# The 31-tap convolution of a recurrent block: all eight tiles on TensorE, in 32x32 diagonal blocks that GpSimd makes

## What is computed

```python
h = rms_norm(x, pre_mix_norm)
p_r, p_k, p_v, p_c, z_rwkv, z_conv = split(h @ w_in)          # w_in: 1024 x 7168
u, gate = split(p_c)
c = u * sigmoid(gate)                                         # 256 x 1024
c = conv(c, dw) + dw_b          # depthwise and causal: c[t, f] = sum_s dw[30 - s, f] * c[t - s, f], 31 taps
y_conv = silu(layer_norm(c)) @ w_conv_out
y_rwkv = recurrence(p_r, p_k, p_v, h)                         # a state of 64 x 64 per head, 16 heads
x = x + rms_norm((sigmoid(z_rwkv) * y_rwkv + sigmoid(z_conv) * y_conv) @ w_out)
```

## Time and profile before

| | us |
|---|---|
| device time, median of 3 runs | 1477.15 |
| lowest, highest | 1475.12, 1480.46 |
| span of the profiled execution | 1474.3 |
| TensorE busy in it | 1383.9 |
| VectorE, ScalarE, GpSimd busy | 1039.1, 760.6, 138.3 |
| mean granted TensorE clock | 0.964 of full |

### The profile page before, as it was taken

How to read it: one execution, slowest core, us unless ns; L and a number is a source line. 1 busy time by engine, 2 the same in 40 slices (tenths; PEclk the granted TensorE clock), 3 DMA queues, 4 the chain that set the end, 5 groups by cost and what they waited for, 6 DMA issues and landing times.

```text
span 1474.3 us, 30170 instructions
## 1 busy us (share of the span) xinstructions
PE 1383.9 (94%) x12477; PEld 1331.2 (90%) x12477; DVE 1039.1 (70%) x1684; ACT 760.6 (52%) x1256; POOL 138.3 (9%) x147
## 2 busy tenths in 40 slices
PE   6998999997798999998998899999999998899997
PEld 6997988896798999998997699999999888899997
DVE  5769899895686665547598967877455655678843
ACT  4584383335645544445467655444355455554432
POOL 2000000001101211001010002111010100221100
PEclk9999999798899999999999899999999999999999
DMA  7633510120163552853484254554656521555550
GB/s 251 188 101 128 173 57 2 61 87 30 66 201 105 186 185 91 264 192 120 139 249 132 79 172 144 180 191 150 209 163 195 173 86 58 169 174 171 185 187 30
DMA packets 204369, 211.06 MB, mean 143 GB/s; under 512 B 8594, under 2 KB 201898, under 8 KB 204090
## 3 DMA queue, kind: packets, MB, share of 16 engines
q1 hardware_dynamic: 202154, 200.87, 42.2%
q0 software_dynamic: 2000, 8.46, 1.9%
q10 hardware_dynamic: 96, 0.02, 0.0%
HBM read 207.70 MB, written 1.64 MB: 142 GB/s over the span
## 4 chain that ended last, share of the span: by engine, by line
PE 72%; DVE 18%; ACT 5%; issue 2%; DMA 1%; POOL 1%; SPq 0%; DVEq 0%; ACTq 0%; POOLq 0%
PE pb L413 19%; PE pb L415 19%; PE pb L414 19%; DVE w_lo L442 3%; DVE pj L1447 2%; PE pb L1942 1%; DVE sub L1375 1%; PE pb L399 1%; PE pb L2324 1%; ACT w_hi L436 1%; DVE x_lo L1223 1%; DMA raw<-in_ffn_w_down_dram 1%; PE pb L1984 1%; PE pb L2030 1%; PE pb L1931 1%
## 5 line engine op out<-in xcount | busy, mean ns | idle before, releaser
L442 DVE TENSOR_TENSOR w_lo<-raw,w_hi 128x1024 fp32r<-128x1024 f32 (+1 forms) x384 | 471.0, 1229 | 165.7 <-ACT w_hi L436 164.9
L413 PE MATMUL pb<-x_hi,w_hi 128*128 128x256 f32 x1968 | 564.2, 287 | 21.4 <-DVE w_lo L442 12.0
L436 ACT ACTIVATE w_hi<-raw 128x1024 fp32r<-128x1024 f32 (+1 forms) x384 | 394.7, 1040 | 345.3 <-PE pb L415 297.1
L414 PE MATMUL pb<-x_lo,w_hi 128*128 128x256 f32 x1968 | 560.1, 285 | 0.0
L415 PE MATMUL pb<-x_hi,w_lo 128*128 128x256 f32 x1968 | 559.8, 284 | 0.0
L413 PEld LDWEIGHTS pb<-x_hi,w_hi 128*128 128x128 f32 x1968 | 381.0, 194 | 26.5 <-DVE w_lo L442 17.8
L414 PEld LDWEIGHTS pb<-x_lo,w_hi 128*128 128x128 f32 x1968 | 381.1, 194 | 0.2
L415 PEld LDWEIGHTS pb<-x_hi,w_lo 128*128 128x128 f32 x1968 | 381.0, 194 | 0.0
L413 PE MATMUL pb<-act_hi,w_hi 128*128 128x256 f32 x528 | 149.6, 283 | 2.6 <-DVE w_lo L442 2.6
L415 PE MATMUL pb<-act_hi,w_lo 128*128 128x256 f32 x528 | 149.4, 283 | 0.0
L414 PE MATMUL pb<-act_lo,w_hi 128*128 128x256 f32 x528 | 149.4, 283 | 0.0
(11 more groups left out here) (312 smaller groups left out, 2109.2 us busy)
## 6 DMA issues: line engine op xcount, KB each, us to landing
raw<-in_ffn_w_up_dram SPq DMA_DIRECT2D x55, 1024.0 KB, 5.0
raw<-in_w_in_dram SPq DMA_DIRECT2D x28, 1024.0 KB, 5.1
raw<-in_ffn_w_down_dram SPq DMA_DIRECT2D x24, 896.0 KB, 4.8
raw<-in_ssd_w_in_dram SPq DMA_DIRECT2D x20, 1024.0 KB, 5.3
raw<-in_fox_w_in_dram SPq DMA_DIRECT2D x16, 1024.0 KB, 5.8
raw<-in_ffn_w_down_dram SPq DMA_DIRECT2D x12, 1024.0 KB, 5.5
raw<-in_ffn_w_gate_dram SPq DMA_DIRECT2D x11, 1024.0 KB, 5.1
raw<-in_ssd_w_out_dram SPq DMA_DIRECT2D x8, 1024.0 KB, 5.1
```

The source lines that it names most:

```text
L413: pe.matmul(o, w_hi[m][:, k, :], hi[:, k0 + k, :], start=first and k == 0, stop=False)
L414: pe.matmul(o, w_hi[m][:, k, :], lo[:, k0 + k, :], start=False, stop=False)
L436: act.activation(w_hi[m][:, 0:nk, :], raw[s][:, 0:nk, m * P:(m + 1) * P], ACT.Copy).then_inc(sem("w_hi_ready"), 1)
L442: dve.tensor_tensor(w_lo[m][:, 0:nk, :], raw[s][:, 0:nk, m * P:(m + 1) * P], w_hi[m][:, 0:nk, :].bitcast(F32), ALU.subtract).then_inc(sem( ...
```

## The change

The convolution no longer runs on VectorE at all, and no longer as 128x128 diagonals on TensorE.

- A 128x128 diagonal holds 128 useful numbers. It is replaced by blocks of 32x32, each a diagonal of 32 features, at row group a (of 4) and column group c (of 4) of the array. For that the features of u and gate are laid out otherwise: tile c of a unit of 512 features holds, on partitions 32a to 32a+31, the features 128a + 32c + i. So 16 blocks (a, c) take four tiles through one tap, and block (a, c) adds to bank 4 + a, partitions of column group c, where the features come out in their usual order. There are 31 taps x 16 blocks x 2 halves = 992 products.
- The blocks are made by GpSimd, 8 instructions (`tap_weights`), each of 8 (or 7) taps x 4 x 32 = 1024 (896) elements per partition: the product of a small identity and the taps' parameters, both read by broadcast. Two are made after `PAIRS_MADE`, ahead of GpSimd's two transfers, six after `GLU_MADE`; there are four buffers (in slots A and GATE), so from the fifth on each waits for the products of four groups before.
- TensorE runs all 992 products after `GLU_MADE` and ahead of the inverses, after a new wait for the first two `z` evacuations, which VectorE now does first. ScalarE only copies the eight sums (`conv_half`), to slot U.
- VectorE's `conv_taps` and ScalarE's diagonals (93 instructions) are gone. `scale_keys(1)` and the loop's other work stay.
- The layer `ug` reads its weight blocks with runs of 32 columns; the first block of a unit needs both halves of the load, and the buffer is freed as a whole after the fourth block, where each half was freed after its two.
- The rows of the convolution's parameters are loaded in the new order: 8 transfers with runs of 32 values instead of 2 with runs of 128. GpSimd makes the small identity at the start, 4 copies of 32x32.

```diff
         def raw_block(ly, s, nk, m):
+            if ly.name == "ug":
+                return raw[s][:, 0:nk, :].rearrange("p k (a c i) -> p k a c i", c=QUARTERS, i=CHUNK)[:, :, :, m, :]
+            return raw[s][:, 0:nk, m * P:(m + 1) * P]
@@ GpSimd
+            def tap_weights(i):
+                h, b = divmod(i, TAP_GROUPS)
+                t0, t1 = tap_range(b)
+                c0 = col["conv_dw"]
+                w = par[:, c0 + KC * t0:c0 + KC * t1].rearrange("p (t k) -> p t k", k=KC)[:, :, QUARTERS * h:QUARTERS * h + QUARTERS]
+                shape = [P, t1 - t0, QUARTERS, CHUNK]
+                if i >= 4:
+                    pool.wait_ge(sem("tap_summed"), i - 3)
+                pool.tensor_tensor(tap_blocks(i)[:, 0:t1 - t0], ident_q[:, :].unsqueeze(1).unsqueeze(1).broadcast_to(shape),
+                                   w.unsqueeze(3).broadcast_to(shape), ALU.mult).then_inc(sem("tap_ready"), 1)
+            pool.wait_ge(sem("dve_stages"), PAIRS_MADE)
+            for i in range(2):
+                tap_weights(i)
             pool.wait_ge(sem("lab_ready"), NCHUNK)
...
+            pool.wait_ge(sem("dve_stages"), GLU_MADE)
+            for i in range(2, 2 * TAP_GROUPS):
+                tap_weights(i)
             pool.wait_ge(sem("dve_stages"), INVERSES_MADE)
@@ ScalarE
+            def conv_half(h):
+                act.wait_ge(sem("tap_summed"), TAP_GROUPS * (h + 1))
+                for a in range(QUARTERS):
+                    k = QUARTERS * h + a
+                    act.activation(slot(CV)[:, k, :], pb[4 + a][:, 0:T], ACT.Identity, bias=par_col("conv_b", k)).then_inc(sem("conv_ready"), 1)
@@ VectorE
+            z_evac(0, Z_EARLY)
             substitute(done + 1, (done + SUB_TOTAL) // 2)
-            z_evac(0, Z_EARLY)
             z_rests(BANKS, BANKS + Z_EARLY)
             substitute((done + SUB_TOTAL) // 2, SUB_TOTAL)
...
-            conv_taps(0, DVE_EARLY - 3)
             scale_keys(1)
-            conv_taps(DVE_EARLY - 3, DVE_EARLY)
...
-                conv_taps(DVE_EARLY + sum(DVE_TAPS[:c]), DVE_EARLY + sum(DVE_TAPS[:c + 1]))
@@ TensorE
             pe.wait_ge(sem("dve_stages"), GLU_MADE)
-            for k in range(PE_TILES):
-                if k >= 2:
-                    pe.wait_ge(sem("conv_ready"), k - 1)
-                for s in range(CONV_TAPS):
-                    pe.wait_ge(sem("tap_ready"), CONV_TAPS * k + s + 1)
-                    mm(pb[4 + k % 2][:, s:T], diag[(CONV_TAPS * k + s) % NDIAG], slot(U)[:, k, 0:T - s],
-                       start=s == 0, stop=s == CONV_TAPS - 1, skip_group_check=True).then_inc(sem("tap_summed"), 1)
-            pe.wait_ge(sem("conv_ready"), PE_TILES)
+            z_out(Z_EARLY)
+            for i in range(2 * TAP_GROUPS):
+                h, b = divmod(i, TAP_GROUPS)
+                t0, t1 = tap_range(b)
+                pe.wait_ge(sem("tap_ready"), i + 1)
+                for tap in reversed(range(t0, t1)):
+                    shift = CONV_TAPS - 1 - tap
+                    for a in range(QUARTERS):
+                        if h and shift == 0:
+                            pe.wait_ge(sem("conv_ready"), a + 1)
+                        for c in range(QUARTERS):
+                            ins = mm(pb[4 + a][quarter[c], shift:T], tap_blocks(i)[quarter[a], tap - t0, c, :],
+                                     slot(U)[quarter[a], QUARTERS * h + c, 0:T - shift],
+                                     start=shift == 0, stop=tap == 0, skip_group_check=True)
+                ins.then_inc(sem("tap_summed"), 1)
+            pe.wait_ge(sem("conv_ready"), KC)
```

More of the change, by code:

```diff
@@ L72, in params_of @@
         n = flat.shape[0] // P
-        out.append((name, n, flat.rearrange("(n p) -> n p", p=P)))
+        rows = flat.rearrange("(n p) -> n p", p=P)
+        if name == "conv_dw":
+            rows = flat.rearrange("(n a c i) -> n c a i", a=QUARTERS, c=QUARTERS, i=CHUNK)
+        out.append((name, n, rows))
     return out
@@ L139, in build, with tap_range, tap_blocks @@
         y_lo = nc.alloc_sbuf_tensor_at("y_lo", [P, KC, T], F32R, offset=arena_base + 8 * (BK + 1) * T * 4)
-        PE_TILES, NDIAG, DIAG_LEAD = 3, 12, 8
-        diag = [slot(ZC)[:, i // 2, P * (i % 2):P * (i % 2) + P] for i in range(NDIAG)]
+        CV, LN_TMP = U, GATE
+        TAP_GROUPS = -(-CONV_TAPS // TAP_GROUP)
+        def tap_range(b):
+            return max(0, CONV_TAPS - TAP_GROUP * (b + 1)), CONV_TAPS - TAP_GROUP * b
+        def tap_blocks(i):
+            v = slot((A, GATE)[i % 4 // 2])[:, 4 * (i % 2):4 * (i % 2) + 4, :].rearrange("p a b -> p (a b)")
+            return v.rearrange("p (t c i) -> p t c i", c=QUARTERS, i=CHUNK)
         Z_EARLY, Z_CHUNK = 2, 2
-        DVE_TAPS = (4, 4, 3, 3, 3, 3)
-        DVE_EARLY = CONV_TAPS - sum(DVE_TAPS)
         LAB_BLOCK, SUB_BLOCK, SUB_STEPS = 5, 9, 2
@@ L320, in build @@
                     ly.free[half].append(occupant[s][half])
-                    occupant[s][half] = ("w_lo_ready", item + M_PER_UNIT // 2 * (half + 1))
+                    occupant[s][half] = ("w_lo_ready", item + (M_PER_UNIT if ly.name == "ug" else M_PER_UNIT // 2 * (half + 1)))
                 unit += 1
@@ L430, in act_head @@
                 act.wait_ge(sem(f"landed{s}{half}"), nth(ly, u, p, ly.landed[half]))
+                if ly.name == "ug" and half == 0:
+                    act.wait_ge(sem(f"landed{s}1"), ly.landed[1][u])
             if ly.name == "lora_in" and m == 2:
@@ L624, in _ @@
                 rows = slice(32 * b, 32 * b + 32)
+                link(pool.tensor_copy(ident_q[rows, :], ident[rows, rows]))
                 link(pool.tensor_copy(g_mask[rows, 0:CHUNK], tri[rows, rows]))
@@ L879, in _ @@
                 z_head(j)
[L880 to L885, removed]
+            for h in range(2):
+                conv_half(h)
             for i in range(CHUNK // INV_GROUP):
@@ L1436, in _ @@
             dve.nop().then_inc(sem("dve_stages"), 1)
-            def conv_taps(first, last):
-                for s in range(first, min(last, CONV_TAPS)):
-                    for k in range(PE_TILES, KC):
-                        w = par_col("conv_dw", KC * (CONV_TAPS - 1 - s) + k)
-                        o, c = slot(GATE)[:, k, :], slot(U)[:, k, :]
-                        if s == 0:
-                            go(ts(o, c, w, par_col("conv_b", k), ALU.mult, ALU.add))
-                        else:
-                            go(stt(o[:, s:T], c[:, 0:T - s], w, o[:, s:T], ALU.mult, ALU.add))
-                    sync()
             def mask_products(c):
```

56 lines of the change are left out of this document (25 added, 31 removed).

## The result

The change made the kernel slower: the median of four runs is 1503.28 us (1500.25 to 1507.48), against 1478.81 us (1475.12 to 1480.81) for the kernel before on the same chip. The ratio of the runs is 1.018, with a 95% interval of 1.015 to 1.021 (the two medians alone give 1.0165). The forecast was 1472.5 with a range of 1461 to 1489; the sign was wrong too. The profiled execution of the changed kernel has a span of 1498.5 us, 24.2 more than before.

The account below looks back on a forecast made before the run. VectorE bounds before the loop, TensorE's convolution up to the inverses, TensorE in the loop with waits and clock. Loop -7.9, inverses -1.2, first two blocks +4.0, parameters +0.5: -4.6 us, 1472.5; range 1461 to 1489.

Parts of the forecast that it names:

- TensorE's convolution: After `GLU_MADE`: 1984 records at 0.41 to 0.49 us a tap, 25 to 30 us, reaching the inverses at 219 to 224.
- Rival C: Tap products start only every 22 ns, as in L2094: 44 us, inverses at 237.7, sum +6.4 us, 1483.6; chance 0.13.
- Parameters: At the kernel's start: six more load issues on SyncE's queue delay TensorE's turns of the parameters by 0.5 us.
- The two early blocks: After `PAIRS_MADE`, at 127.2 us: two GpSimd blocks hold up VectorE's products, 4.0 us later; bounds 0 and 8.8.
- GpSimd's instruction: Each tap block of 1024 elements on GpSimd takes 2.3 us, at 2.1 ns an element; bounds 2.3 and 4.6.
- Rival B: GpSimd's blocks take 4.6 us each: sum +14.0 us, 1491.2; chance 0.14.
- Six late blocks: After `GLU_MADE`: six GpSimd blocks cost VectorE's slabs 8.2 us; `INVERSES_MADE` at 226.6, inverses start 1.2 us sooner.
- The loop: Chunk loop without VectorE's multiply-adds: TensorE's 2.8 us of waits and part of its time at 1.2 GHz vanish, gain 7.9 us.
- Edits at nothing: Parts counted as costing nothing, such as ScalarE's lost diagonals, later `ug` loads and 32-column runs in the splits.

Follow-up runs that it names:

- the bursts of 64 columns: The changed kernel with each tap product after the unshifted one over 64 columns instead of 226 to 255: taps 54 us against 55, span 1494.8 us.
- the first pair of profiles: The first profile each of the kernel before and the changed kernel: loop 114.8 and 107.8 us; in the second profiles 111.9 and 112.1 us.

## Why the prediction was wrong, step by step

- *TensorE's convolution* is the step that failed. It took the pace of 7.5 to 15 ns from bursts of 32 records and asked only whether the array could hold it for 1984. Nothing in the sum asked whether the instructions would come. They come at 14 ns each, 28 ns a record with its load, so 1984 records take 55.5 us, not 25 to 30. With that the path was wrong too: the forecast had the inverses wait for VectorE's substitution (226.6, measured 228.8), and they waited for the taps, until 253.9. The taps started 1.0 us after the GLU, where 0.8 was forecast.
- Of the forecast's 0.41 to 0.49 us a tap of four tiles, bursts at full width took 2.3 us for four taps, 0.57. That alone would have made 36 us: the array's pace was sized too short as well, beside the supply that was left out.
- *Rival C* had the direction, and its row, L2094 at 22 ns, was the nearest to the truth; it was given 0.13 because L2112 was faster. But a run of 32 says nothing of a run of 1984. With C's 9.8 us replaced by the measured 26.0 - 6.7 = 19.3, its sum is 0.5 + 4.0 + 19.3 - 7.9 = +15.9. The Trainium skill's floor of about 25 ns (TensorE: Matmul & The Clock Gate, Wait — 56ns, not 53.3ns?) is near the average of 28; as a floor it doesn't hold here, since records come 13 ns apart inside the bursts of 64 columns.
- *Parameters*: 0.5 forecast, bounds 0 and 2.3, measured 4.0. The step took the duration of an issue from transfers with whole rows, 0.39; with runs of 32 values it was 0.73 in the median, eight times, so SyncE's next parameter load was issued 5.5 us later (20.0 against 14.5), and TensorE waited 2.8 us for the last of them.
- *The two early blocks*: 4.0 forecast, 2.7 measured, mechanism right. VectorE's L463 took 2.99 us and its next large product (L1381) 3.67:

```profile
131.26 2.99 DVE L463 TENSOR_TENSOR w_lo<-raw,w_hi 128x1024 fp32r<-128x1024 f32 x1
```

- *GpSimd's instruction*: 2.3 forecast; 1.9 where VectorE didn't come between, 2.6 in the median. Rival B, 4.6 us, is excluded.
- *Six late blocks*: 8.2 us on VectorE forecast, 3.8 measured, all of it gone with the blocks. Two came at once and four one by one, each after a wait for TensorE's products; that fewer met a slab product for this reason is my reading, no run tests it. It lay off the path.
- *The loop*: -7.9 forecast, -7.1 in the first pair of profiles, 0 in the second, -4.7 by the ratio of the kernel without VectorE's taps. The forecast took one profile's stretches at 1.2 GHz as the kernel's own. Its 2.8 us of waits stand (2.7 and 4.2 at like clock); its 5.1 us from the clock don't, since the stretch of 13.6 us is missing in the kernel before's second profile as well. That -7.1 came so near is luck.
- *Edits at nothing*: right for `ug`, whose 32-column runs and later loads add nothing between 151 and 180 us (6.7 us behind at both). The tail was taken as unchanged; it differed by 1.8 to 5.2 us.

By the terms as measured: 4.0 + 2.7 + 19.3 - 7.1 + 5.2 = 24.1 us, and 24.2 between the spans.

## What to carry to other kernels

Splitting a product into many small ones for the places of the array multiplies the instructions: count two for each record (it has its weight load), and ask at what pace a long run of instructions has come in the trace, not a run of 32. Here 256 instructions came every 3.6 us, so in a long run records worth less than 28 ns of array time gain nothing by being shorter; 64x64 blocks took four tiles through in 26.8 us with half the instructions of the 28.3 us in 32x32 blocks. And a stage on the critical path that gets 11 us shorter gives that only if what comes next isn't bound by another engine's total work.

## What the runs showed that I had not expected

- The pace of TensorE's instructions is independent of what they do: mostly 3.46 or 3.74 us a block of 256, with 241 columns at 2.4 GHz or 64 at 1.2.
- Four GpSimd instructions in a row let one VectorE instruction wait for three of them (7.25 us for 1.2), where single ones had cost it one turn each. Spread over waits for TensorE, six cost 3.8 us in all.
- The same 124 KB of parameters cost SyncE two issues of 0.37 us as whole rows and eight of 0.73 (medians) in runs of 32 values.
- ScalarE's copy of 64 partitions of a PSUM bank to another half of the partitions took 0.47 us, the same as one of all 128, and 16 copies of 32 partitions held TensorE for 7.9 us.
